# More homes for the gathered value rows of a token-routed layer: a ring of six grows by one to four rows

## The reference, cut to what matters

```python
def peer_ffn(h, w_q, sub_keys, u, v):          # per block of 128 tokens
    q = (xt @ w_q).reshape(TOKEN_BLOCK, PEER_HEADS, 2, PEER_HALF_DIM)
    sc = jnp.einsum('thcd,chnd->thcn', q, sub_keys)
    top_s, top_i = lax.top_k(sc, 16)           # per half; then the 16 best pairs: expert, share
    ...                                        # out = sum over experts of gelu(h . u[e]) * share * v[e]
x = x + peer_ffn(rms_norm(x, ffn_norm[l]), peer_w_q[l], peer_sub_keys[l], peer_u[l], peer_v[l])
x = second_block(x, c_2, w_ada_2, ...)         # attention mixers and a gated MLP
```

## Time and profile before

| | us |
|---|---|
| runs of the kernel | 2606.09, 2613.95, 2614.55 (median 2613.95) |
| the profiled execution, its own time | 2616.31 |
| span of its trace | 2614.5 |
| first to last gather issued | 365.1 to 1931.6 |

### The profile page before, as it was taken

How to read it: one execution, slowest core, us unless ns; L and a number is a source line. 1 busy time by engine, 2 the same in 40 slices (tenths; PEclk the granted TensorE clock), 3 DMA queues, 4 the chain that set the end, 5 groups by cost and what they waited for, 6 DMA issues and landing times. The chain is left out here.

```text
span 2614.5 us, 25392 instructions
## 1 busy us (share of the span) xinstructions
PE 2108.2 (81%) x7625; PEld 1332.7 (51%) x7625; DVE 1729.6 (66%) x3556; ACT 605.2 (23%) x1394; POOL 1033.1 (40%) x1083
## 2 busy tenths in 40 slices
PE   4985867797776977777897877876969798899999
PEld 4963544454332433343543433332429664788777
DVE  4856438887787767767676787787757462544465
ACT  2134213342232121112211232222211221111121
POOL 0000015666666666766665666667630000000000
PEclk8995888898887988898998988889989787899999
DMA  4741037999999999999999999999974200333222
GB/s 175 274 169 65 17 129 273 345 365 348 329 359 388 370 370 393 405 382 384 372 395 368 404 388 360 358 360 369 369 261 161 82 1 13 106 93 94 79 81 96
DMA packets 266857, 676.48 MB, mean 259 GB/s; under 512 B 25725, under 2 KB 114162, under 8 KB 266738
## 3 DMA queue, kind: packets, MB, share of 16 engines
q0 software_dynamic: 147456, 536.94, 54.2%
q1 hardware_dynamic: 119282, 138.13, 15.9%
HBM read 672.87 MB, written 2.10 MB: 258 GB/s over the span
## 5 line engine op out<-in xcount | busy, mean ns | idle before, releaser
L2189 PE MATMUL bank<-arena 128*128 128x512 f32 x1536 | 814.8, 666 | 162.3 <-DMA arena<-in_peer_v,arena 81.7
L2419 DVE SCALAR_TENSOR_TENSOR arena<-arena,h_ps 128x1024 f32<-128x1024 f32 x512 | 612.4, 1216 | 145.4 <-DMA arena<-in_peer_u,arena 108.5
L2152 POOL DMA_INDIRECT arena<-in_peer_v,arena x512 | 507.4, 991 | 351.8 <-issue 140.3
L2152 POOL DMA_INDIRECT arena<-in_peer_u,arena x512 | 510.4, 997 | 218.0 <-issue 143.2
L2189 PEld LDWEIGHTS bank<-arena 128*128 128x128 f32 x1536 | 306.0, 212 | 513.3 <-issue 373.5
L2432 DVE SCALAR_TENSOR_TENSOR x<-arena,x 128x1024 f32<-128x1024 f32 x128 | 164.8, 1287 | 45.6 <-DMA arena<-in_peer_v,arena 24.8
L2273 ACT ACTIVATE arena<-ident,arena 128x128 f32<-128x128 f32 x384 | 136.0, 393 | 58.1 <-issue 24.2
L1453 PE MATMUL bank<-hT,arena 128*128 128x256 f32 x512 | 125.6, 400 | 23.1 <-DMA arena<-in_peer_w_q 14.2
L142 DVE CAST parts<-arena 128x2048 fp32r<-128x2048 f32 (+4 forms) x60 | 68.1, 1136 | 113.0 <-DMA arena<-in_w_gate_up 72.0
L144 DVE TENSOR_TENSOR parts<-arena,parts 128x2048 fp32r<-128x2048 f32 (+4 forms) x60 | 126.6, 2111 | 4.5
L1453 PEld LDWEIGHTS bank<-hT,arena 128*128 128x128 f32 x512 | 102.6, 202 | 52.4 <-issue 23.9
(11 more groups left out here) (413 smaller groups left out, 3444.4 us busy)
## 6 DMA issues: line engine op xcount, KB each, us to landing
arena<-in_w_in SPq DMA_DIRECT2D x16, 1536.0 KB, 6.7
arena<-in_w_ada SPq DMA_DIRECT2D x12, 2048.0 KB, 10.3
arena<-in_w_gate_up SPq DMA_DIRECT2D x44, 512.0 KB, 4.9
arena<-in_peer_w_q SPq DMA_DIRECT2D x16, 1024.0 KB
arena<-in_w_down SPq DMA_DIRECT2D x22, 512.0 KB, 3.5
arena<-in_peer_u,arena POOLq DMA_INDIRECT x512
arena<-in_peer_v,arena POOLq DMA_INDIRECT x512
arena<-in_w_in SPq DMA_DIRECT2D x8, 1024.0 KB
```

Of the source, the lines that this page charges most:

```text
L2152: nc.gpsimd.indirect_dma_start(out=ring[:, n % R, :], out_offset=None, in_=a[table][0], in_offset=bass.IndirectOffsetOnAxis(ap=expert[:, s ...
L2189: ins = nc.tensor.matmul(psum[half][:, :], diag[:, m % R, :], v_ring[:, n % R, half * 512:(half + 1) * 512], start=(s % PH == 0 and j == 0 ...
L2419: nc.vector.scalar_tensor_tensor(out=u_ring[:, n % R, :], in0=u_ring[:, n % R, :], scalar=1.0, in1=h_ps[:, :], op0=ALU.mult, op1=ALU.mult, ...
```

## The change

The v rows no longer go round six tiles. A table `V_HOMES` lists twelve homes with the slots [first, end) in which each may be filled: the six ring tiles always; the four tiles of `rows`, each from the slot at which `place_h` has read it (6 slots after its copy stands in the program), tiles 0 and 1 only up to slot 258; and the first half of `hT_flat` as two tiles, from slot 86 to slot 262. For each position the home with the oldest use is taken, so the homes that are free are used in turn. Worked out from the table, the distance back to the row whose use is waited for is 6 before and now:

| slots | homes | distance |
|---|---|---|
| 23 to 85 | ring, rows 0 | 7 |
| 88 to 133 | and both halves of hT | 9 |
| 135 to 259 | and rows 1 | 10 |
| 269 to 389 | ring, rows 2 | 7 |
| 391 to 527 | and rows 3 | 8 |

Of 512 v rows 132 land outside the ring. The first fill of a new home waits for `h_placed` or `q_summed` in place of a row's use. Two places of ScalarE's program get a wait for the last v row that lay in the tile they write. Each home has a semaphore of its own for arrival.

```diff
+        PLACED = 6
+        V_HOMES = [(v_ring[:, i, :], PK, (STEPS + 1) * PK) for i in range(R)]
+        V_HOMES += [(rows[:, tb, :], (tb * PH) * PK + PLACED + (PK if tb == 0 else 0), (C0 - PK if tb < 2 else (STEPS + 1) * PK))
+                    for tb in range(TB)]
+        V_HOMES += [(hT_flat[:, i * D:(i + 1) * D], 5 * PK + PLACED, C0 - PK + 4) for i in range(2)]
+        v_in = [sem(f"v_in{i}") for i in range(len(V_HOMES))]
+        v_home, v_prev, v_turn, v_last = [], [], [], [None] * len(V_HOMES)
+        for n in range(STEPS * PK):
+            free = [i for i, (_, first, end) in enumerate(V_HOMES) if first <= n + PK < end]
+            i = min(free, key=lambda i: -1 if v_last[i] is None else v_last[i])
+            v_home.append(i)
+            v_prev.append(v_last[i])
+            v_turn.append(v_home.count(i))
+            v_last[i] = n
+
+        def await_v_row(engine, n):
+
+            if on_dve(n):
+                engine.wait_ge(v_taken, dve_count(n + 1))
+            else:
+                engine.wait_ge(v_used, pe_count(n + 1))
+
+        def await_v_home(pool, n):
+
+            if v_prev[n] is not None:
+                await_v_row(pool, v_prev[n])
+            elif v_home[n] >= R + TB:
+                pool.wait_ge(q_summed, 2 * PH)
+            elif v_home[n] >= R:
+                pool.wait_ge(h_placed, v_home[n] - R + 1)
...
         def block2_act(act, slot):
             if slot in (0, 1):
+                await_v_row(act, v_last[R + slot])
                 act.wait_ge(y_added, slot + 1)
...
                 k = slot - 7
+                if k % 4 == 0:
+                    await_v_row(act, v_last[R + TB + k // 4])
                 act.wait_ge(b_turned, 2 * KD + k + 1)
...
                         if i >= 1:
-                            last = (i - 1) * PK + j - R
-                            if last >= 0:
-                                if on_dve(last):
-                                    pool.wait_ge(v_taken, dve_count(last + 1))
-                                else:
-                                    pool.wait_ge(v_used, pe_count(last + 1))
-                            gather("peer_v", v_ring, v_in, i - 1, j)
+                            n = (i - 1) * PK + j
+                            await_v_home(pool, n)
+                            gather("peer_v", V_HOMES[v_home[n]][0], v_in[v_home[n]], i - 1, j)
...
                     for half in range(2):
                         ins = nc.tensor.matmul(psum[half][:, :], diag[:, m % R, :],
-                                               v_ring[:, n % R, half * 512:(half + 1) * 512],
+                                               V_HOMES[v_home[n]][0][:, half * 512:(half + 1) * 512],
```

More of the change, by code:

```diff
@@ L1412, in program @@
         u_in = [sem(f"u_in{i}") for i in range(R)]
-        v_in = [sem(f"v_in{i}") for i in range(R)]
         u_used, v_used, pre_ready, gelu_ready = sem("u_used"), sem("v_used"), sem("pre_ready"), sem("gelu_ready")
@@ L1425, in program @@
         N4_0 = O1_0 + 17
+        C0 = 17 * PK + 3
         DVE_J = (2, 6, 10, 14)
@@ L1474, in copy_scores @@
             nc.scalar.copy(sc[:, :, Q % PH, :], qs_ps[:, :].rearrange("p (i n) -> p i n", i=2)).then_inc(sc_copied, 1)
-        C0 = 17 * PK + 3
         SM_QK = 2 * SM_W
@@ L2148, in _, with gather @@
                 nc.gpsimd.iota(iota16_i, [[1, PK]], base=0, channel_multiplier=0).then_inc(iota_ready, 1)
-                def gather(table, ring, arrived, s, j):
-                    n = s * PK + j
+                def gather(table, row, arrived, s, j):
                     nc.gpsimd.indirect_dma_start(
-                        out=ring[:, n % R, :], out_offset=None, in_=a[table][0],
+                        out=row, out_offset=None, in_=a[table][0],
                         in_offset=bass.IndirectOffsetOnAxis(ap=expert[:, s % TB, j:j + 1], axis=0),
-                    ).then_inc(arrived[n % R], 16)
+                    ).then_inc(arrived, 16)
                 for i in range(STEPS + 1):
@@ L2167, in _ @@
                             after(pool, u_used, i * PK + j - R + 1)
-                            gather("peer_u", u_ring, u_in, i, j)
+                            n = i * PK + j
+                            gather("peer_u", u_ring[:, n % R, :], u_in[n % R], i, j)
                         if i >= 1:
-                            last = (i - 1) * PK + j - R
-                            if last >= 0:
-                                if on_dve(last):
-                                    pool.wait_ge(v_taken, dve_count(last + 1))
-                                else:
-                                    pool.wait_ge(v_used, pe_count(last + 1))
-                            gather("peer_v", v_ring, v_in, i - 1, j)
+                            n = (i - 1) * PK + j
+                            await_v_home(pool, n)
+                            gather("peer_v", V_HOMES[v_home[n]][0], v_in[v_home[n]], i - 1, j)
             @block.tensor
@@ L2184, in values @@
                         after(pe, y_added, tb)
-                    pe.wait_ge(v_in[n % R], 16 * (n // R) + 16)
+                    pe.wait_ge(v_in[v_home[n]], 16 * v_turn[n])
                     m = pe_count(n)
@@ L2429, in add_value @@
                     n, tb = s * PK + j, s // PH
-                    dve.wait_ge(v_in[n % R], 16 * (n // R) + 16)
+                    dve.wait_ge(v_in[v_home[n]], 16 * v_turn[n])
                     dve.drain()
-                    nc.vector.scalar_tensor_tensor(out=x[:, tb, :], in0=v_ring[:, n % R, :], scalar=coef[:, s % 2, j:j + 1],
+                    nc.vector.scalar_tensor_tensor(out=x[:, tb, :], in0=V_HOMES[v_home[n]][0], scalar=coef[:, s % 2, j:j + 1],
                                                    in1=x[:, tb, :], op0=ALU.mult, op1=ALU.add).then_inc(v_taken, 1)
```

## The result

| | before | changed |
|---|---|---|
| median us | 2604.81 (20 runs, 2581.07 to 2620.46) | 2613.62 (20 runs, 2597.15 to 2631.76 and one of 8875.12) |
| profiled execution, its own time | 2616.31 | 2619.94 |
| its span | 2614.5 | 2618.1 |

Changed to before is 1.0044, interval [1.0024, 1.0063]; the run of 8875 us is not in it. In sum: from 0.4% slower to 0.3% faster; the two small gains, some 7 us each, are clear of noise and stand on the quicker sort of chip.

A forecast was written before the change was run, and what follows sets the result against it. The prediction took VectorE's and TensorE's waits for gathered rows as the loss, after 781 us, with attention setting the pace before. Terms 0 + 9 + 4 + 3 + 6 = 22 us less gave 2592 us, range 2560 to 2615.

The forecast's parts named there:

- the zero up to slot 134: Gather stage, 434 to 781 us: 0 us gained, since attention sets the pace and nobody waits for gathered rows.
- the terms 9, 4, 3 and 6: Us saved in gather windows 781-1159, 1159-1552, 1552-1850 and 1850-1940 us, mostly from rows in hand at 1.28 us each.
- POOL's waits only change their name: Rival, gather stage: v waits become u waits, the u ring still six; 2606 to 2614 us, chance 0.26.
- The forecast sign: Sign of being right, gather stage: VectorE's wait for u rows falls by a quarter.
- upper ends: Most the middle windows could gain at 410 GB/s throughout: 22 us (781-1159 us) and 24 us (1159-1552 us).
- The 2.80 us wait: POOL's wait before one v gather in the last step, claimed to go, worth 2.5 us.
- The 6 us of this term: Gather stage, 1850 to 1940 us: 2.5 us wait gone, 2.6 us rows in hand, a little from the step before.
- the slower rival: Second block's weight tiles, from 1159 us: at least eight of ten come late, 26 us lost, 2618 us; chance 0.08.
- the one of waits that hold POOL: Rival: a wait for `h_placed` or a row of `rows` holds POOL each token block, 10 us each; 2632 us, chance 0.04.
- The other signs: POOL's v idle time 352 to some 200 us; gather stage 15 to 25 us shorter; later stages changing over 5 us unexplained.
- Theories B and C: From the follow-up, gather stage: more gathers ahead lengthen weight loads (1.003 to 1.006); places in `rows` and `hT` themselves cost.

The follow-up runs named there:

- swap6: Kernel before, using the homes outside the ring but closing one ring tile for each in use, so six at any time; quick chip, 2513.74 us, 0.9987.
- changed_fourth: The changed kernel unaltered, measured again on a quick chip against the kernel before (2513.93 us): 2507.19 us, 0.9976.
- v4: Kernel before with the v ring cut to four homes and none outside it; quick chip, 2584.0 us, 1.0272.
- half_v: Kernel before with each v gather 128 x 512 floats in place of 128 x 1024, 134 of 537 MB left out; slow chip, 2593.46 us, 0.9932.
- changed_again: The changed kernel unaltered, measured again on a slow chip against the kernel before (2613.71 us): 2611.33 us, 0.9993.
- half_v_changed: The changed kernel with v gathers of 512 columns in place of 1024; quick chip, against the kernel before: 2437.54 us, 0.9697.

## Why the prediction was wrong

Its own steps, one by one.

**The windows and what bounds them.** The reading that VectorE and TensorE wait for rows in the two middle windows was right for the trace, and so was the zero up to slot 134 (347 us before, 344.7 now). The step that failed is the next one: that rows in hand build up there and that each is worth 1.28 us of the stage. It stands in the terms 9, 4, 3 and 6; the gains measured in the same windows are -2.9, +2.5, and -4.3 for the two last together. What sets the pace in its place is shown on quick chips (VectorE in the first window, POOL in the second, the bytes with POOL close behind in the rest); on slow chips, where the first comparison was made, it stays open.

**Where the rows in hand went.** The prediction gave 1.28 us for each row in hand "each time the queue goes from thin to full", with the u ring still six. It saw the objection and priced it as a rival with 0.26: POOL's waits only change their name. That rival is what happened, and its 2606 to 2614 us hold the measured 2613.62. The slow pair shows it in the section on the result, 115 us less before v gathers and 104 more before u gathers. A pair on quick chips, where the trace names nearly every releaser, is swap6 (six homes) and changed_fourth (7 to 10 homes). POOL's waits, swap6:

```profile
POOL arena L2185 <- PE bank L2219: 93.6, 74, 15.5
POOL arena L2185 <- DVE arena L2449: 69.2, 91, 17.2
...
POOL hT L2185 <- PE bank L2219: 13.8, 13, 3.6
POOL rows L2185 <- PE bank L2219: 11.1, 16, 2.9
```

and changed_fourth:

```profile
POOL arena L2184 <- DVE arena L2448: 135.0, 132, 17.2
...
POOL arena L2184 <- PE bank L2218: 28.0, 33, 12.1
...
POOL rows L2184 <- PE bank L2218: 2.7, 7, 0.8
```

With another 0.9 us of changed_fourth, before gathers into `hT`, waits for rows that TensorE uses fell from 118.5 to 31.6 us, waits for VectorE's dots rose from 69.8 to 135.0: three quarters of what the v waits lost. By all idle time before gathers, v has 249 and 179 us, u 217.5 and 271.2, together 467 and 450; of the 17 us between them 13 went into longer gathers (1023 and 1036 us busy). The prediction held that POOL can barely outrun the DMA, 0.94 + 0.30 = 1.24 us against 1.28. But 0.94 us is the commonest gather; the mean in the earlier trace rows is 0.99 us, so the cadence is 1.29 to 1.30 us, and POOL cannot outrun a DMA that takes a row in 1.28 us. That is a second reason why few rows in hand build up, though no run tests it by itself. The rows that did get ahead only stood in the queue longer, by the page's row of DMA issues (the last number is the median us from issue to landing), swap6, changed_fourth and v4:

```profile
arena<-in_peer_u,arena POOLq DMA_INDIRECT x512, 8.9
```
```profile
arena<-in_peer_u,arena POOLq DMA_INDIRECT x512, 10.3
```
```profile
arena<-in_peer_u,arena POOLq DMA_INDIRECT x512, 6.5
```

Divided by 1.28 us a row, an estimate, 8.9 us are some seven rows on their way and 10.3 us eight. Seven are enough for 409 GB/s in the second window and 396 to 400 in the last three. With four homes 6.5 us are five rows, and v4 lost 70 us. The knee lies between four homes and six, and the change went on from six.

**Why the shorter waits gave nothing.** The forecast sign came: VectorE's wait for u rows fell from 108.5 to 75.9 us, by 30% where a quarter was forecast, and TensorE's for v rows from 81.7 to 43.1 us. The time did not come: all idle time before the dots fell only from 145.4 to 131.5 us, that before TensorE's `values` rose from 162.3 to 177.6 us, and no window became shorter for it. The prediction took a shorter wait for a row as a shorter stage; other waits took its place. The row of before is (the changed kernel's stands in the first fence above):

```profile
L2419 DVE SCALAR_TENSOR_TENSOR arena<-arena,h_ps 128x1024 f32<-128x1024 f32 x512 | 612.4, 1216 | 145.4 <-DMA arena<-in_peer_u,arena 108.5
```

On the quick chips, VectorE waits for u rows with the queue full or with POOL at its own pace, and a home more ends neither wait earlier. Before the dots of swap6 and changed_fourth it waited 164.8 and 157.8 us in the stage, 7 us less; from slot 22 to the last gather the stage took 1402.1 and 1398.0 us. On the slow chips half_v says that bytes pace little of the stage. If so, the DMA's 386 GB/s in the third window of the earlier trace rows was the rate at which the engines asked, and 410 less 386 was hardly anybody's loss; the prediction divided one by the other for its upper ends.

**The last step.** The 2.80 us wait did not go but grew, 3.30 us, and 4.06 us in changed_fourth; around it the changed kernel's timeline shows (start, us, engine, line, idle before; L2455 makes the coefficients, L2302 the diagonals from them):

```profile
1924.89 7.47 PE L2218 MATMUL bank<-arena 128*128 128x512 f32 x16 [3.13 <-DMA arena<-in_peer_v,arena]
...
1925.14 0.18 DVE L2455 TENSOR_TENSOR arena<-arena 128x16 f32<-128x16 f32 x1 [0.33 <-issue]
...
1926.43 2.10 ACT L2302 ACTIVATE arena<-ident,arena 128x128 f32<-128x128 f32 x6
...
1927.78 0.94 POOL L2184 DMA_INDIRECT rows<-in_peer_v,arena  x1 [3.30 <-PE bank L2218]
1928.78 1.28 DVE L2461 SCALAR_TENSOR_TENSOR x<-arena,x 128x1024 f32<-128x1024 f32 x1 [3.46 <-DMA arena<-in_peer_v,arena]
```

The 3.10 and the 3.46 us of the earlier trace rows stand there again, as 3.13 and 3.46. The values of the last step need the coefficients of the whole step before, which are made at 1925.14 us; its first diagonal comes at 1926.43. By then POOL has filled the homes that were free and waits until TensorE has used the last row of the step before. No ring makes the coefficients come earlier. The 6 us of this term were wrong in kind, not in size.

**The weight tiles.** L1994 waited once, 18.1 us, where L1964 waited once, 15.7 us; the slower rival's eight late tiles of ten did not come. This rival is refuted, as is the one of waits that hold POOL: no row of the gathers' waits in changed_fourth, where the releasers are named, has ScalarE (which counts `h_placed`) in it. The rival's sum was also off: 26 us lost and 18 gained from 2614 are 2622, not 2618.

**The other signs.** POOL's idle time before v gathers fell to 237 us, not to some 200. From first to last gather the stage took 1566.5 us before and 1577.1 now, longer and not 15 to 25 us shorter. What follows the last gather took 7.5 us less (682.9 and 675.4), which the prediction called a sign of an error; but it takes 672 to 688 us in the traces of all kernels here, so this says nothing.

**The pages.** The Trainium skill, Perfetto Trace Analysis, section Optimization Strategy, says that the same gap repeating on the engine that should be saturated can mean too few buffers. The runs agree with it at four homes (1.027) and hardly at six: the 198 us of such gaps in the slow trace were worth nothing there, and on quick chips the homes gave 7 us. A gap of the engine that issues says only that somebody else has the next row's place. The Trainium skill, DMA: Bandwidth & Descriptors, section Where 436 GB/s comes from, gives about 358 GB/s as the limit of HBM for one core; swap6's five windows at 387 to 409 GB/s stand above it, with one core running.

**The first comparison's 0.4%.** It is not explained. In the second set the ratio was 0.9993 [0.9968, 1.0017], whose interval does not reach 1.0024 to 1.0063, and no window of the profile lost more than 4.3 us. Between these two comparisons the changed kernel's median hardly moved (2613.62 and 2611.33); that of the kernel before did (2604.81 and 2613.71). Theories B and C, which would have made a loss, both fell in runs on quick chips; no run was made to separate them on slow ones. In the first comparison's trace TensorE's waits for the query weights are longer (10.6 us before, 18.3 now), as B wants, but not in changed_again's (10.9), and there the wait for a tile of `w_in_2` is 15.5 us, as before. It stays open.

## What to carry to other kernels

Waits of the engine that issues gathers say how deep the ring is, not what a deeper ring would give. Ask first whether the queue is full (the rate in a short window, the time from issue to landing divided by the time of one row), whether the issuing engine's own time per gather leaves it room to get ahead, and whether anyone would start earlier; a run with the bytes cut by a known amount tells whether the bytes set the pace before a ring is lengthened. Of two rings that one engine serves in turn, the longer was worth little more than the shorter here.

## What the runs showed of the hardware that was not expected

**Two sorts of chips.** The kernel before takes 2514 to 2515 us on three chips and 2605 to 2614 us in two comparisons. No chip served in two sets, so this may also be a state that a chip is in for a time. Nearly all of it lies in the gather stage: of the 106 us between the spans of the profiles (2614.5 before, 2508.3 swap6) the five windows of the stage hold 98 (1498 and 1399.6). The same hand-over shows it, TensorE's last matmul of an attention unit (L1222) to VectorE (L1230), in the waits within the stage, the kernel before on a slow chip and swap6 on a quick one:

```profile
DVE recip L1230 <- remote: 20.2, 6, 5.1
```
```profile
DVE recip L1230 <- PE bank L1222: 1.1, 1, 1.1
```

Six waits of up to 5.1 us against one of 1.1 (two more in the slow trace, 3.3 us in sum, are put down to L1222 by name). In the slow trace the six are put down to "remote": the record of the sender's count is missing. In one case TensorE's matmul ended by 660.76 us and VectorE began at 668.69, after 4.06 us with nothing else to do:

```profile
659.98 0.78 PE L1222 MATMUL bank<-arena,hT 128*128 128x64 f32 x6
...
668.69 0.16 DVE L1230 RECIPROCAL recip<-total 128x1 f32<-128x1 f32 x1 [4.06 <-remote]
```

Waits put down to "remote" stand in the gather stage of every slow trace and of no quick one. Whether the signals are late or only their records are missing, and why on some chips only, was not tried and stays open; that engines wait for one another there rather than for rows agrees with half_v. Another difference was not tried as a cause either: the granted TensorE clock is 0.91, 0.86, 0.87, 0.91 and 0.90 in the five windows before and 0.95, 0.96, 0.91, 0.94 and 0.93 in swap6, and TensorE is busy 1182 and 1147 us in them, 35 of the 98 us between the stages.

**GpSimd is nearly the limit itself.** Its gathers are 1017.8 us of busy time and 1024 x 0.30 us between them, 1325 us, of a stage that takes 1566 us from first to last issue in the profile before and 1401 us in half_v_changed. An estimate from this: below about 1325 us no ring, byte or weight would bring it while a gather takes POOL as long as here.
